# Making the four q units of the sparse attention in the fixed front part and keeping them in DRAM

## The chip, the cores and the metric

The kernel is one program on one core of a Trainium2 chip. The metric is the device time of one execution in microseconds (us). The engines are TensorE (PE, with its weight loads as PEld), VectorE (DVE), ScalarE (ACT), GpSimd (POOL) and SyncE (SP), which here issues most of the DMAs.

## The reference

A transformer block with three parallel mixers and a second block of two layers, all in float32, for 512 tokens of width 1024. What the change touches is the sparse attention (NSA) of the first block and the mLSTM beside it:

```
h = rmsnorm(x, g_pre_mix[l])
z = h @ w_in[l]
q_nsa, kv_nsa, g_nsa, qkv_ml, if_ml, o_ml, q_mem, g_merge = jnp.split(z, offsets, axis=-1)
q = q_nsa.reshape(B, S, NSA_GROUPS, NSA_HPG, NSA_DH)          # 4 groups x 4 heads x 64
o_cmp, p_cmp = nsa_compressed(q, kv[:, :, 0], kv[:, :, 1], ...)  # scores against 31 compressed keys
o_slc = nsa_selected(q, kv[:, :, 2], kv[:, :, 3], top_i, top_ok)
o_win = nsa_window(q, kv[:, :, 4], kv[:, :, 5])
y_nsa = gb[..., 0:1] * o_cmp + gb[..., 1:2] * o_slc + gb[..., 2:3] * o_win
...
h_ml = mlstm_chunkwise(q_m, k_m, v_m, i_pre, logf)            # 4 heads of 128
h_ml = h_ml * lax.rsqrt(jnp.mean(h_ml * h_ml, axis=-1, keepdims=True) + EPS) * ml_head_g
y_ml = jax.nn.sigmoid(o_ml) * h_ml
...
gm = jax.nn.sigmoid(g_merge.reshape(B, S, N_BRANCH, D_MODEL))
y = gm[:, :, 0] * (y_nsa @ w_proj_nsa) + gm[:, :, 1] * (y_ml @ w_proj_ml) + gm[:, :, 2] * (y_mem @ w_proj_mem)
```

## The kernel before, in words

**Units.** Every matrix product goes in units of 256 weight columns. SP loads the unit's weights (1 MB) into one of two buffers `w_raw`; ACT copies them, rounded, to `w_hi`; POOL (DVE in later parts) subtracts to get `w_lo`; PE then makes hi*hi, lo*hi and hi*lo, 48 matmuls of 512 columns for a feature-major unit. Each buffer has two halves that alternate, and every engine does its part in program order: ACT and DVE run the same list of steps as PE, and where a step waits, what stands behind it on that engine waits too.

**The front.** `UNITS` are 22 fixed units (memory keys, compressed, selected and window keys and values, gates, then 14 to 17 `qk`, 18 and 19 `v`, 20 and 21 `o` of the mLSTM). `SCHEDULE` is the order, written by hand, of these units and the steps of the mixers between them. For each mLSTM head h there are `ml_scores` (PE makes one broadcast and four score matmuls; ACT and DVE turn each into decayed, masked scores; the third and fourth matmul wait for the first and second to be masked), `ml_out` (PE, 10 matmuls; DVE makes the reciprocal of the denominator, ACT scales and squares; `m_h` is then counted up, for which the next head's `ml_scores` waits), `ml_gain` and `ml_norm` (two heads each; ACT root, DVE 8 multiplications, `m_y`), and last `ml_turn` (PE turns the result by 16 transposes; ACT and DVE split it into `yml`, counted by `m_lo_s`).

**The loop over 4 groups.** Each turn uses four units: one q unit and three units of the merge gates (two tiles of 128 columns each). PE first makes the q unit (`products`), then 18 of the 144 gate matmuls (`GATE_PRE`), waits until ACT and DVE have split q into `q_stacked` (`q_split`), makes 32 small matmuls against the compressed keys, then 35 attention steps with 3 gate matmuls in each (`GATE_STEP`), then the tail: it turns the compressed probabilities (`c_t`), makes 12 gate matmuls, 16 outputs of the compressed branch, the gate matmuls that are left, and turns `y_tok` when DVE has it ready (`y_done`). `q_stacked` lies in the place of `qk_in`, the key tiles `k_st` in that of `o_ml`.

Of the kernel before, what the change touches and what calls it, by code (L numbers as in the profile page):

```python
# [13 lines left out]
P = 128  # L14
T = 512
# [33 lines left out]
for _name, _count in ROWS:  # L49
# [9 lines left out]
         ("in", C_V, UC, "v"), ("in", C_V + UC, UC, "v"), ("in", C_O, UC, "o"), ("in", C_O + UC, UC, "o")]  # L59
NFIX = len(UNITS)  # L60
FEATURE_MAJOR = ("mem_k", "q_mem", "kc", "vc", "ks", "kw", "qk")
# [7 lines left out]
for _h in range(4):  # L69
    SCHEDULE += [("mem_scores", _h), ("unit", 6 + 2 * _h), ("mem_turn", _h), ("unit", 7 + 2 * _h), ("mem_out", _h)]  # L70
    if _h in (1, 2):
# [3 lines left out]
             ("ml_scores", 0), ("ml_out", 0), ("unit", 19), ("ml_scores", 1), ("ml_out", 1),  # L75
             ("unit", 20), ("ml_gain", 0), ("ml_norm", 0), ("unit", 21), ("ml_scores", 2), ("ml_out", 2), ("ml_scores", 3),
             ("ml_gain", 1), ("ml_out", 3), ("ml_norm", 1), ("ml_turn", 0)]
# [29 lines left out]
GATE_PRE, GATE_STEP = 18, 3  # L107
GATE_EVAC = {8: 0, 16: 1, 24: 2, 32: 3}
# [38 lines left out]
NSA_PER = 31  # L147
# [70 lines left out]
def build(nc, A, const_in, invcount_in, out):  # L218
    with ExitStack() as ctx:
# [48 lines left out]
        kcmp = at("k_cmp", [P, GROUPS, NC], PE0 + 8 * KB + 768)  # L268
# [41 lines left out]
        d_ml = [at(f"decay{i}", [P, T], WK + (41 + 2 * i) * KB - 512) for i in range(2)]  # L310
# [17 lines left out]
        q_st = at("q_stacked", [P, HPG, T], WK, F32R)  # L328
        k_st = [[at(f"k_{name}_{part}_twice", [P, T], WK + (30 + 4 * b + 2 * i) * KB, F32R)
# [54 lines left out]

        g_scratch = nc.dram_tensor("gate_scratch", [GATE_TILES * GROUPS, P, T], F32, kind="Internal").ap()
# [69 lines left out]
        q_high = sem("q_first_high_ready")  # L455
        q_split = sem("q_split_ready")
# [102 lines left out]
        def _(sp):  # L559
# [29 lines left out]
            sp.wait_ge(k_stored, 64)  # L589
            with sp.Fori(0, GROUPS) as g:  # L590
                def gate_load(b):
                    load(g * 2 + (U_NSA // 2 + (b + 1) // 2), (b + 1) % 2, w_in_t[:, :, bass.ds(g * UC + (C_MERGE + b * D), UC)], KT, UC)

                load(g * 2 + U_NSA // 2, 0, w_in_t[:, :, bass.ds(g * UC, UC)], KT, UC)
                gate_load(0)
                gate_load(1)
# [8 lines left out]
                gate_load(2)  # L605
# [57 lines left out]
        def _(act):  # L663
            chain = Chain(act_chain_s)

            def high_in_loop(u2, s, slot):

                act.wait_ge(w_landed[s], u2 * 16 + 16)
                act.wait_ge(w_used, u2 * 2 + (s - 1))
                nc.scalar.activation(w_hi[slot][:, :], raw[s][:, :], ACT.Copy).then_inc(w_hi_ready, 1)  # L670
# [73 lines left out]
            def evacuate(u):  # L744
# [40 lines left out]
                if kind == "qk":  # L785

                    for j in range(2 * (u - 14), 2 * (u - 14) + 2):
# [65 lines left out]
            def ml_turn(_):  # L853
                for h in range(4):
                    act.wait_ge(m_turned, h + 1)
                    nc.scalar.activation(yml[0][:, h, :], bank[h][:, :], ACT.Copy).then_inc(m_hi_s, 1)
# [4 lines left out]
                     "ml_turn": ml_turn}  # L861
# [15 lines left out]
            with act.Fori(0, GROUPS) as g:  # L877
                high_in_loop(g * 2 + U_NSA // 2, 1, 1)
                act.wait_ge(w_used, g * 4 + (U_NSA + 1))
                for h in range(2):  # L880
                    half = slice(DH * h, DH * (h + 1))
                    nc.scalar.activation(q_st[half, h, :], bank[0][half, :], ACT.Copy).then_inc(q_high, 1)
# [28 lines left out]
                for i in range(NS + 2):  # L911
# [19 lines left out]
                ins.then_inc(c_ta, 1)  # L931
                gate_evac(4)
# [218 lines left out]
        def _(pe):  # L1151
# [1184 lines left out]
```

## Time and profile before

| | |
|---|---|
| median of 3 runs | 3069.28 us (3068.79 to 3071.99) |
| the profiled execution | 3068.96 us, span 3067.1 us, mean granted TensorE clock 0.971 |
| PE busy | 2897.8 us, 94% of the span |
| DVE, ACT, POOL busy | 1455.8, 895.2, 333.9 us |
| chain that ended last | PE 72%, issue 16%, POOL 5%, DVE 3% |

The clock column of the views is the share of full speed that TensorE was granted: 1.00 is 2.4 GHz, 0.50 is 1.2 GHz. Idle time in a view is the time that an engine stood before an instruction, with the instruction that released it behind the arrow.

### The profile page before, as it was taken

The page shows a single profiled execution, that of the slowest core. Times are in us where ns is not written, and L with a number is a line of the kernel's source. Part 1 is how long each engine was busy: PE and PEld are TensorE (multiplying, and loading weights), DVE is VectorE, ACT ScalarE, POOL GpSimd, SP SyncE. Part 2 cuts the span into 40 slices and gives each one's busy share as a digit, 9 for nine tenths or more (in the row PEclk, how much of TensorE's full clock was granted, in tenths as well). Part 3 has the DMA queues.
Part 4 walks back from the last instruction along what each step waited for, and adds up shares of the span by engine and source line. Part 5 has one row for each costly group of instructions (what it writes and reads, how often), then busy time and mean ns, then how long its engine had stood idle before and what let it go on. Part 6 is the DMA issues. An engine that isn't in the chain of part 4 may idle for free.

```text
span 3067.1 us, 34757 instructions
## 1 busy us (share of the span) xinstructions
PE 2897.8 (94%) x13510; PEld 2378.6 (78%) x13510; DVE 1455.8 (47%) x2131; ACT 895.2 (29%) x1222; POOL 333.9 (11%) x64
## 2 busy tenths in 40 slices
PE   6988799999899999999999999999999889899997
PEld 6777688888777888778888888878888765588886
DVE  2334354444457453375433644344453389454532
ACT  4333443334233221232222422122222231422221
POOL 4322112111310000000000000000000065100000
PEclk9998899999999999999999999999999999999999
DMA  6222112221442223322232222332222221223222
GB/s 192 91 63 69 55 42 73 80 75 45 147 142 71 96 96 103 103 69 96 96 115 71 91 96 96 103 103 82 96 96 88 77 69 42 69 71 102 95 91 72
DMA packets 255086, 270.55 MB, mean 88 GB/s; under 512 B 5695, under 2 KB 243407, under 8 KB 254858
## 3 DMA queue, kind: packets, MB, share of 16 engines
q1 hardware_dynamic: 250688, 261.87, 26.5%
q10 hardware_dynamic: 4298, 7.36, 0.7%
q8 instruction: 61, 1.00, 0.1%
q14 instruction: 39, 0.32, 0.0%
HBM read 258.72 MB, written 10.49 MB: 88 GB/s over the span
## 4 chain that ended last, share of the span: by engine, by line
PE 72%; issue 16%; POOL 5%; DVE 3%; ACT 2%; DMA 1%; SPq 0%; POOLq 0%; ACTq 0%; DVEq 0%
PE bank L1164 21%; PE bank L1165 21%; PE bank L1166 21%; POOL w_lo L1127 3%; POOL w_lo L1121 3%; PE bank L1658 1%; PE bank L1179 1%; PE bank L1180 1%; PE bank L1181 1%; ACT w_hi L678 1%; PE bank L1192 1%; PE bank L1194 1%; PE bank L1193 1%; PE bank L1309 0%; DVE rstd L2090 0%
## 5 line engine op out<-in xcount | busy, mean ns | idle before, releaser
L1164 PE MATMUL bank<-h_hi,w_hi 128*128 128x512 f32 x2064 | 814.0, 394 | 43.2 <-POOL w_lo L1127 24.6
L1165 PE MATMUL bank<-h_lo,w_hi 128*128 128x512 f32 x2064 | 808.9, 392 | 0.0
L1166 PE MATMUL bank<-h_hi,w_lo 128*128 128x512 f32 x2064 | 808.6, 392 | 0.0
L2046 DVE TENSOR_TENSOR w_lo<-w_raw,w_hi 128x2048 fp32r<-128x2048 f32 (+1 forms) x174 | 386.8, 2225 | 423.3 <-ACT w_hi L678 363.8
L1164 PEld LDWEIGHTS bank<-h_hi,w_hi 128*128 128x128 f32 x2064 | 391.4, 190 | 132.4 <-POOL w_lo L1127 28.8
L1165 PEld LDWEIGHTS bank<-h_lo,w_hi 128*128 128x128 f32 x2064 | 391.1, 190 | 81.9 <-issue 1.2
L1166 PEld LDWEIGHTS bank<-h_hi,w_lo 128*128 128x128 f32 x2064 | 390.8, 189 | 82.2
L678 ACT ACTIVATE w_hi<-w_raw 128x2048 fp32r<-128x2048 f32 (+2 forms) x120 | 218.5, 1825 | 459.8 <-PE bank L1166 412.5
L1164 PE MATMUL bank<-hid_hi,w_hi 128*128 128x512 f32 x880 | 343.4, 390 | 0.0
L1166 PE MATMUL bank<-hid_hi,w_lo 128*128 128x512 f32 x880 | 342.4, 389 | 0.0
L1165 PE MATMUL bank<-hid_lo,w_hi 128*128 128x512 f32 x880 | 342.4, 389 | 0.0
L1127 POOL TENSOR_TENSOR w_lo<-w_raw,w_hi 128x2048 fp32r<-128x2048 f32 x34 | 216.8, 6380 | 1088.4 <-ACT w_hi L678 1088.3
L670 ACT ACTIVATE w_hi<-w_raw 128x2048 fp32r<-128x2048 f32 x114 | 217.8, 1911 | 337.6 <-PE bank L1166 330.1
L971 ACT ACTIVATE gate_tmp<-gate_tmp 128x512 f32<-128x512 f32 x110 | 67.7, 632 | 492.2 <-DVE gate_tmp L2137 492.2
L1164 PEld LDWEIGHTS bank<-hid_hi,w_hi 128*128 128x128 f32 x880 | 165.2, 188 | 34.6 <-issue 0.5
L1165 PEld LDWEIGHTS bank<-hid_lo,w_hi 128*128 128x128 f32 x880 | 165.2, 188 | 34.6 <-issue 0.5
L1166 PEld LDWEIGHTS bank<-hid_hi,w_lo 128*128 128x128 f32 x880 | 165.2, 188 | 34.4
L2145 DVE TENSOR_TENSOR gate_tmp<-gate_tmp,bank 128x512 f32<-128x512 f32 x110 | 75.6, 687 | 238.8 <-PE bank L1166 236.8
L2137 DVE TENSOR_TENSOR gate_tmp<-bank,rstd 128x512 f32<-128x512 f32 x110 | 70.9, 686 | 189.2 <-PE bank L1166 188.9
L1121 POOL TENSOR_TENSOR w_lo<-w_raw,w_hi 128x2048 fp32r<-128x2048 f32 x24 | 110.1, 4591 | 435.0 <-ACT w_hi L670 435.0
L888 ACT ACTIVATE prob<-prob,nsa_stat 128x512 f32<-128x512 f32 (+3 forms) x128 | 71.8, 561 | 157.9 <-DVE nsa_stat L1968 157.9
L1968 DVE CUSTOM_DVE_ANT_0 prob<-bank,const_masks 128x512 f32<-128x512 f32 (+3 forms) x128 | 62.8, 491 | 113.5 <-PE bank L1430 72.5
(366 smaller groups left out, 3431.2 us busy)
## 6 DMA issues: line engine op xcount, KB each, us to landing
w_raw<-in_ffn_w_in_dram SPq DMA_DIRECT2D x88, 1024.0 KB, 5.1
w_raw<-in_w_in_dram SPq DMA_DIRECT2D x32, 1024.0 KB, 5.3
w_raw<-in_ffn_w_out_dram SPq DMA_DIRECT2D x32, 1024.0 KB, 4.9
w_raw<-in_w_ffn_in_dram SPq DMA_DIRECT2D x22, 1024.0 KB, 5.1
w_raw<-in_ffn_w_out_dram SPq DMA_DIRECT2D x16, 768.0 KB, 4.3
w_raw<-in_conv_w_pw_dram SPq DMA_DIRECT2D x12, 1024.0 KB, 5.3
w_raw<-in_w_ffn_down_dram SPq DMA_DIRECT2D x8, 1024.0 KB, 4.9
gate_scratch<-gate_stage ACTq DMA_DIRECT2D x24, 256.0 KB, 2.0
```

The lines of the kernel that those rows point to most:

```text
L670: nc.scalar.activation(w_hi[slot][:, :], raw[s][:, :], ACT.Copy).then_inc(w_hi_ready, 1)
L678: nc.scalar.activation(w_hi[SLOT[u]][:, 0:n], raw[s][:, 0:n], ACT.Copy).then_inc(w_hi_ready, 1)
L888: nc.scalar.activation(prob[i % 4][:, 0:n], prob[i % 4][:, 0:n], ACT.Exp, bias=nmax[:, i:i + 1], scale=-1.0, accum_out=psum_row[:, i:i + 1 ...
L971: nc.scalar.activation(tg[t][:, :], tg[t][:, :], ACT.Silu).then_inc(silu_done, 1)
L1121: nc.gpsimd.tensor_tensor(w_lo[s][:, :], raw[s][:, :], w_hi[s][:, :].bitcast(F32), ALU.subtract).then_inc(w_lo_ready, 1)
L1127: nc.gpsimd.tensor_tensor(w_lo[d][:, :], raw[u % 2][:, :], w_hi[d][:, :].bitcast(F32), ALU.subtract).then_inc(w_lo_ready, 1)
L1164: nc.tensor.matmul(bank[b][:, 0:n], wh, xh, start=first, stop=False)
L1165: nc.tensor.matmul(bank[b][:, 0:n], wh, xl, start=False, stop=False)
L1166: ins = nc.tensor.matmul(bank[b][:, 0:n], wl, xh, start=False, stop=last)
L2046: v.tensor_tensor(w_lo[slot][:, 0:n], raw[s][:, 0:n], w_hi[slot][:, 0:n].bitcast(F32), ALU.subtract).then_inc(w_lo_ready, 1)
L2137: v.tensor_tensor(tg[t][:, :], bank[b + t][:, :], rb[:, :], ALU.mult).then_inc(g_scaled, 1)
L2145: mark(v.tensor_tensor(tg[t][:, :], tg[t][:, :], bank[b + 2 + t][:, :], ALU.mult), up_read, n + (t + 1))
```

## The change

The four q units become fixed units 19, 21, 23 and 25 of the front, between the v and o units. PE makes each of them between an `ml_scores` and its `ml_out` (the fourth between the last `ml_out` and `ml_turn`). ACT and DVE split them into a new buffer `q_stage`, and ACT's queue stores each to DRAM (`q_scratch`, 1 MB). SP loads one back into `q_stacked` per group as soon as the group before has turned its compressed probabilities. The loop's units are now two full gate units and two halves of one (128 columns each), and its turn begins with the small matmuls against the compressed keys, with one gate matmul behind each pair. The split of a group's compressed keys moves from the head of its turn into the turn before, the first group's ahead of `ml_out` of the last head. The core of the diff:

```diff
-         ("in", C_V, UC, "v"), ("in", C_V + UC, UC, "v"), ("in", C_O, UC, "o"), ("in", C_O + UC, UC, "o")]
+         ("in", C_V, UC, "v"), ("in", 0, UC, "q"), ("in", C_V + UC, UC, "v"), ("in", UC, UC, "q"),
+         ("in", C_O, UC, "o"), ("in", 2 * UC, UC, "q"), ("in", C_O + UC, UC, "o"), ("in", 3 * UC, UC, "q")]
...
-             ("ml_scores", 0), ("ml_out", 0), ("unit", 19), ("ml_scores", 1), ("ml_out", 1),
...
+             ("ml_scores", 0), ("unit", 19), ("ml_out", 0), ("q_store", 0), ("unit", 20), ("ml_scores", 1), ("unit", 21), ("ml_out", 1),
...
-GATE_PRE, GATE_STEP = 18, 3
-GATE_EVAC = {8: 0, 16: 1, 24: 2, 32: 3}
+GATE_CMP, GATE_STEP = 1, 3
+GATE_EVAC = {6: 0, 13: 1, 21: 2, 29: 3}
...
@@ SP
+            sp.wait_ge(q_stored, 16)
+            sp.wait_ge(sT_ready, 4 * TT)
+            sp.sem_inc(c_t, 1)
...
-                sp.wait_ge(y_split, g * 2 + 2)
+                gate_load(0, 0, 0, UC)
+                gate_load(0, 1, D, UC)
+
+                sp.wait_ge(c_t, g + 1)
+                sp.dma_start(q_st[:, :, :].rearrange("p h t -> p (h t)").bitcast(F32),
+                             q_scratch[bass.ds(g, 1), :, :].rearrange("a p n -> p (a n)")).then_inc(q_landed, 16)
+                sp.wait_ge(m_y, 16)
...
+                gate_load(1, 0, 2 * D, P)
+                gate_load(1, 1, 2 * D + P, P)
@@ ACT
+            def q_store(n):
+                u = UNIT_OF["q"][n]
+                act.wait_ge(evac_act, u + 1)
+                act.wait_ge(evac_dve, DVE_EVACS[u + 1])
+                act.dma_start(q_scratch[n], q_stage[:, :, :].rearrange("p h t -> p (h t)").bitcast(F32)).then_inc(q_stored, 16)
...
-                act.wait_ge(c_t, g + 1)
+                act.wait_ge(c_t, g + 2)
...
                 ins.then_inc(c_ta, 1)
+                high_in_loop(g * 2 + (U_NSA // 2 + 2), 0, 0)
                 gate_evac(4)
@@ PE
-            pe.wait_ge(m_lo_s, 4)
...
+                        if m < 2:
+                            pe.wait_ge(m_lo_s, m + 1)
...
-                products(0, KT, UC, (h_hi, h_lo), (0, 1))
-                gates(GATE_PRE)
-                pe.wait_ge(q_split, g + 1)
...
+                pe.wait_ge(q_landed, g * 16 + 16)
+                pe.wait_ge(kc_ready, g + 1)
...
+                        gates(GATE_CMP)
@@ DVE
+                elif kind == "q":
+                    if TURN_OF[u] > 0:
+                        dve.wait_ge(q_stored, 16 * TURN_OF[u])
+                    halves = (slice(0, DH), slice(DH, P))
+                    for h in range(2):
+                        link(v.tensor_scalar(q_stage[halves[h], 2 + h, :], b1[halves[h], :], 1.0, None, ALU.mult))
+                    for h in (2, 3, 0, 1):
+                        if h == 0:
+                            dve.wait_ge(evac_act, u + 1)
+                        own, other = halves[h % 2], halves[1 - h % 2]
+                        ins = v.tensor_tensor(q_stage[other, h, :], bank[2 * (u % 2) + h // 2][own, :],
+                                              q_stage[own, h, :].bitcast(F32), ALU.subtract)
```

On ACT, at the end of the front, the rows of the kernel before run from the last head's output (`h_ml`) over the root and the four copies of `ml_turn` to the loop:

```order
L839 ACTIVATE h_ml<-bank,stat 128x128 x4
L841 ACTIVATE ml_junk,stat<-h_ml 128x128 x4
L849 ACT_TABLE_LOAD
L849 ACTIVATE stat<-stat 128x4x2
L856 ACTIVATE yml_hi<-bank 128x512 x4
L877 UNCONDITIONAL_BRANCH
```

and of the changed kernel at the same place:

```order
L863 ACTIVATE h_ml<-bank,stat 128x128 x4
L865 ACTIVATE ml_junk,stat<-h_ml 128x128 x4
L873 ACT_TABLE_LOAD
L873 ACTIVATE stat<-stat 128x4x2
L696 ACTIVATE w_hi<-w_raw 128x2048
L803 ACTIVATE q_stage<-bank 64x512 x2
L886 DMA q_scratch<-q_stage 128x2048
L880 ACTIVATE yml_hi<-bank 128x512 x4
```

Between the root and the copies there now stand the next unit's `w_hi`, the fourth q unit's two copies and its store.

On PE, at the head of the loop's turn, the kernel before has the last of the 18 gate matmuls and then 32 small ones in a row, of which the first rows are

```order
L1403 MATMUL bank<-h_hi,w_lo 128x512
L1424 REGISTER_ALU
L1429 MATMUL bank<-k_cmp_high,q_stacked 128x32
L1430 MATMUL bank<-k_cmp_low,q_stacked 128x32
L1429 MATMUL bank<-k_cmp_high,q_stacked 128x32
L1430 MATMUL bank<-k_cmp_low,q_stacked 128x32
```

and the changed kernel has, behind the 16 transposes of `ml_turn`,

```order
L1403 MATMUL bank<-identity_ones,h_ml 128x128 x16
L1414 UNCONDITIONAL_BRANCH
L1414 ISA
L1453 REGISTER_ALU
L1449 MATMUL bank<-k_cmp_high,q_stacked 128x32
L1450 MATMUL bank<-k_cmp_low,q_stacked 128x32
L1422 ISA
L1426 ISA
L1430 MATMUL bank<-h_hi,w_hi 128x512
L1449 MATMUL bank<-k_cmp_high,q_stacked 128x32
L1450 MATMUL bank<-k_cmp_low,q_stacked 128x32
L1430 MATMUL bank<-h_lo,w_hi 128x512
```

The q unit is gone from the head of the turn, and a gate matmul of 512 columns stands behind each small pair.

## Rows read from the trace of the kernel before

**Rows 1.** The page, part 1.

```profile
PE 2897.8 (94%) x13510; PEld 2378.6 (78%) x13510; DVE 1455.8 (47%) x2131; ACT 895.2 (29%) x1222; POOL 333.9 (11%) x64
```

**Rows 2.** Windows: from head 0's scores to the first group's attention.

```profile
core 0: us, PE busy (x) PEld busy (x) DVE busy (x) ACT busy (x) POOL busy (x), PEclk, DMA share, GB/s
271.50:391.70 120.20, 95.14 (x524) 78.68 (x523) 44.26 (x107) 42.10 (x90) 21.26 (x5) 0.84 0.18 53
```

**Rows 3.** Waits of PE in 271 to 392 us: total, times, longest.

```profile
PE bank L1378 <- DVE h_ml L1890: 7.8, 1, 7.8
PE bank L1357 <- DVE s_ml L1865: 5.3, 6, 1.4
PE bank L1368 <- DVE s_ml L1865: 4.5, 4, 1.2
PE bank L1352 <- ACTq L844: 4.5, 1, 4.5
PE bank L1164 <- DVE yml_lo L1896: 1.8, 1, 1.8
PE bank L1429 <- DVE q_stacked L1926: 1.1, 1, 1.1
```

**Rows 4.** Windows of lowered clock (columns as in rows 2).

```profile
277.30:284.90 7.60, 6.68 (x33) 6.68 (x34) 1.62 (x8) 0.84 (x3) 0.00 (x0) 0.55 0.22 77
342.60:355.50 12.90, 9.96 (x22) 5.36 (x23) 6.28 (x13) 3.50 (x13) 0.00 (x0) 0.50 0.00 0
362.90:373.00 10.10, 5.74 (x17) 4.57 (x18) 5.24 (x15) 5.36 (x7) 1.61 (x1) 0.50 0.13 37
390.40:396.90 6.50, 6.50 (x19) 5.28 (x20) 2.82 (x7) 1.63 (x4) 0.00 (x0) 0.50 0.00 0
489.50:495.50 6.00, 6.00 (x22) 5.33 (x22) 1.53 (x4) 0.81 (x2) 0.00 (x0) 0.50 0.00 0
591.70:594.60 2.90, 2.90 (x8) 2.30 (x7) 1.32 (x4) 0.81 (x2) 0.00 (x0) 0.50 0.00 0
567.80:571.00 3.20, 3.20 (x11) 2.26 (x10) 2.37 (x13) 0.57 (x1) 0.00 (x0) 0.50 0.25 89
```

**Rows 5.** Window of the q unit of group 1 (columns as in rows 2).

```profile
470.92:481.92 11.00, 11.00 (x52) 9.10 (x51) 2.63 (x4) 3.21 (x2) 4.60 (x1) 1.00 0.52 150
```

**Rows 6.** Timeline of DVE and POOL: start, duration, what, idle before.

```profile
321.96 6.57 DVE L1890 SCALAR_TENSOR_TENSOR h_ml<-h_ml,stat,o_ml 128x128 f32<-128x128 f32 x8
323.51 4.61 POOL L1127 TENSOR_TENSOR w_lo<-w_raw,w_hi 128x2048 fp32r<-128x2048 f32 x1 [5.69 <-ACT w_hi L678]
356.90 0.35 DVE L1872 COPY stat<-bank 128x2 f32<-128x2 f32 x2 [2.89 <-PE bank L1368]
363.24 2.19 DVE L1890 SCALAR_TENSOR_TENSOR h_ml<-h_ml,stat,o_ml 128x128 f32<-128x128 f32 x8
818.24 9.47 POOL L1121 TENSOR_TENSOR w_lo<-w_raw,w_hi 128x2048 fp32r<-128x2048 f32 x2 [15.92 <-ACT w_hi L670]
823.22 0.68 DVE L2028 TENSOR_TENSOR merge_gate<-merge_gate,bank 128x512 f32<-128x512 f32 x1
```

**Rows 7.** Timeline of DVE: the split of the first q unit.

```profile
382.78 1.41 DVE L1922 TENSOR_SCALAR q_stacked<-bank 64x512 fp32r<-64x512 f32 x2
384.33 2.94 DVE L1926 TENSOR_TENSOR q_stacked<-bank,q_stacked 64x512 fp32r<-64x512 f32 x4
```

**Rows 8.** Timeline: the tail of group 0 on ACT, DVE and PE.

```profile
457.17 1.92 ACT L670 ACTIVATE w_hi<-w_raw 128x2048 fp32r<-128x2048 f32 x1 [0.71 <-ACT gate_stage L906]
460.31 2.03 ACT L929 ACTIVATE pT_cmp<-bank 31x512 f32<-31x512 f32 x4 [1.23 <-PE bank L1480]
466.85 3.16 DVE L2009 SCALAR_TENSOR_TENSOR y_tok<-bank,nsa_stat,y_tok 128x64 f32<-128x64 f32 x16 [7.66 <-PE bank L1487]
470.07 1.09 PE L1494 MATMUL bank<-identity_ones,y_tok 128*128 128x128 f32 x8 [1.07 <-DVE y_tok L2009]
```

**Rows 9.** The page, part 6: KB of each DMA and us to landing.

```profile
w_raw<-in_w_in_dram SPq DMA_DIRECT2D x32, 1024.0 KB, 5.3
```

More of the change, by code:

```diff
@@ L74 @@
              ("ml_const", 0), ("ml_rows", 0), ("unit", 15), ("unit", 16), ("unit", 17), ("ml_cols", 0), ("unit", 18),
-             ("ml_scores", 0), ("ml_out", 0), ("unit", 19), ("ml_scores", 1), ("ml_out", 1),
-             ("unit", 20), ("ml_gain", 0), ("ml_norm", 0), ("unit", 21), ("ml_scores", 2), ("ml_out", 2), ("ml_scores", 3),
-             ("ml_gain", 1), ("ml_out", 3), ("ml_norm", 1), ("ml_turn", 0)]
+             ("ml_scores", 0), ("unit", 19), ("ml_out", 0), ("q_store", 0), ("unit", 20), ("ml_scores", 1), ("unit", 21), ("ml_out", 1),
+             ("q_store", 1), ("unit", 22), ("ml_scores", 2), ("unit", 23), ("ml_out", 2), ("q_store", 2), ("ml_gain", 0), ("ml_norm", 0),
+             ("unit", 24), ("ml_scores", 3), ("ml_gain", 1), ("first_keys", 0), ("ml_out", 3), ("ml_norm", 1), ("unit", 25), ("q_store", 3), ("ml_turn", 0)]
 U_NSA = NFIX
@@ L143 @@
 K_END = 1656
-NSA_PER = 31
+NSA_PER = 25
 class Chain:
@@ L309, in build @@
         conv_acc = [at(f"conv_acc{i}", [P, T], AR + (58 + 2 * i) * KB) for i in range(2)]
-        d_ml = [at(f"decay{i}", [P, T], WK + (41 + 2 * i) * KB - 512) for i in range(2)]
+        d_ml = [at(f"decay{i}", [P, T], WK + (41 + 2 * i) * KB) for i in range(2)]
         head_g = at("head_g", [P, T], AR + 56 * KB)
@@ L785, in evacuate @@
                 if kind == "qk":
-                    for j in range(2 * (u - 14), 2 * (u - 14) + 2):
+                    for j in range(2 * TURN_OF[u], 2 * TURN_OF[u] + 2):
                         act.wait_ge(conv_done, j + 1)
@@ L855, in ml_turn @@
                     act.wait_ge(m_turned, h + 1)
[L856 removed]
+                    nc.scalar.activation(yml[0][:, h, :], bank[ML_TURN_BANK[h]][:, :], ACT.Copy).then_inc(m_hi_s, 1)
+            def q_store(n):
[3 more added lines that the diff above has]
+                act.dma_start(q_scratch[n], q_stage[:, :, :].rearrange("p h t -> p (h t)").bitcast(F32)).then_inc(q_stored, 16)
             steps = {"mem_scores": mem_scores, "mem_turn": mem_turn, "mem_out": mem_out, "cmp_hidden": cmp_hidden,
@@ L878, in _ @@
                 high_in_loop(g * 2 + U_NSA // 2, 1, 1)
[L879 to L882, printed above, removed]
                 def exp_step(i):
@@ L1777, in unit @@
                     dve.wait_ge(evac_act, u + 1)
-                    for j in range(2 * (u - 14), 2 * (u - 14) + 2):
+                    for j in range(2 * TURN_OF[u], 2 * TURN_OF[u] + 2):
                         acc = conv_acc[j % 2][:, :]
@@ L1904, in _ @@
                     steps[what](n)
-            dve.wait_ge(mask_in_place, 16)
-            for i in range(2):
-                link(v.memset(kc_st[i][:, :].bitcast(F32), 0.0))
             dve.sem_inc(y_split, 2)
```

144 lines of the change are left out of this document (78 added, 66 removed).

## The prediction

> **What bounds the kernel now.** I read the page's busy times first: PE is busy 94% of the span, no other engine half of it [rows 1]. So a change pays only by what it takes from PE's idle time or gives back of its clock. The number of matmuls of full width stays the same. The windows show where there is something to take: from head 0's scores to the first group's attention PE is busy 95.1 of 120.2 us at a mean clock of 0.84 [rows 2]. The waits of PE there add up to 25.0 us: 7.8 before `ml_turn` for the normalised heads, 5.3 within `ml_scores` for masked scores, 4.5 before `ml_out` (1.2 for each of heads 0 to 2 and 0.9 for head 3), 4.5 before the last `ml_scores` for ACT, 1.8 at the loop's head for `yml`, 1.1 for the q split [rows 3]. The windows of lowered clock show the second loss: there PE works at 1.2 GHz, so about half of its busy time in each is lost [rows 4].
>
> **What is removed.** Three q units leave this comparison, since they only change place: a q unit takes 11.0 us at full clock [rows 5], in the loop as in the front. I compare the moment at which the compressed scores of group 0 are done, before and after, for the same amount of matmuls.
>
> Idle time taken away, from rows 3: the waits before `ml_out` of heads 0 to 2 (3.6) get a q unit of 11 us over them, and the masks that they wait for come 1.2 us after the scores. The 4.5 before the last `ml_scores` gets an o unit. The 7.8 before `ml_turn` gets the fourth q unit. The 1.1 for the q split of group 0 goes, and so does the 1.8, in which all four parts of `yml` were waited for. Sum 18.8 us. The 5.3 within `ml_scores` stays.
>
> **What comes back as new waits.** ACT and DVE are in order, and now carry more.
>
> *Before the last scores.* The split of a q unit holds DVE for 4.5 us (382.78 to 387.27) [rows 7] before it can take the denominator of `ml_out`. From there to the root took 356.90 to about 363.0, 6.1 us [rows 6]. So after q unit 23 the root comes at 4.5 + 6.1 = 10.6 us. The 8 multiplications of `ml_norm` follow; free of POOL they take 2.19 us, beside POOL's `w_lo` they took 6.57 [rows 6]. In this place ACT makes the next unit's `w_hi` right behind the root, as in the slow case, so they end at about 17.4. PE needs only `ml_out` (2.5) and o unit 24 (some 11.4 us, a little over a q unit) to be at the last scores at 13.9, and DVE's first argument is wanted 1.1 us later. PE waits some 2.4 us for it, with ACT's tables between sigmoid and exponential 3. What was a step without consequence now delays the scores.
>
> *Before `ml_turn`.* From the last `ml_out` to the last multiplication took 356.90 to 365.43, 8.5 us [rows 6]. Now `w_hi` of the loop's first unit stands right behind the root on ACT, and so POOL lies beside the multiplications again: 8.5 + 4.4 = 12.9, less 11.0 of q unit 25: 1.9 us of wait.
>
> *At the loop's head.* DVE splits q unit 25 only then (4.5), ACT's store waits for that split, and ACT's copies for `yml` are queued behind the store: some 0.4 us for the issue, 0.6 for the first copy, 0.7 for DVE's part. That is 6.3 us after the last multiplication, of which PE fills 2.2 with transposes and the first small pair; then its first gate matmul waits 4.1 us. New waits: 3 + 1.9 + 4.1 = 9.0. Idle time net: 18.8 - 9.0 = 9.8 us.
>
> **The clock in this stretch.** Lost before, by rows 4: 3.3 at head 0's scores, the same again at head 1's (a window alike), 5.0 at 342.6, 2.9 at 362.9, 3.3 at 390.4: 17.8 us. In each case PE had stood still or had only sparse matmuls just before. After the change these stretches are followed by dense units, yet the scores with their inner waits stay as they are. I keep 2.5 us for head 0, 2.5 for head 1 and 1 for head 2 (between nothing and the 3.3 seen), 3.5 for the last head with its longer wait, and 2.5 at the loop's head: 12. Gain 6, and between 0 and 13 if these choices are all wrong one way. The front gives 9.8 + 6 = 16.
>
> **The loop's heads of groups 1 to 3.** The q split's 1.1 us goes three times (the same row stands in each group's waits): 3.2. The clock fell behind the 32 small matmuls of each group: 6.0 us busy at half in group 1, 2.9 in groups 2 and 3 alike [rows 4]: 3.0 + 1.45 + 1.45 = 5.9 lost. With a full matmul behind each small pair PE is dense for half of this place; in the short attention steps it is about as dense and its clock holds. I expect most of the 5.9 back, but not surely; the fall in the tail (567.8 to 571.0, 1.6 us lost [rows 4]) stays. I count 8 us of 3.2 + 5.9.
>
> **What is new there, costed at nothing.** The q load is issued at `c_t`, when the transposes of the compressed probabilities are done, at about 460.2 in group 0. PE turns `y_tok` from 470.07 to 471.16 [rows 8], 11 us after `c_t`; a load of 1 MB lands in 5.3 us [rows 9]. Cover 5.5 us; late, it costs what is over, in each of three groups. The key loads behind it have the small matmuls and 16 gate matmuls as well, some 7 us more. The first gate unit's `w_hi` moves from before `c_t` (457.17) to behind ACT's four copies (2.03 us) [rows 8]: 2.1 + 1.9 + 4.6 of POOL puts `w_lo` at 8.7 us after `c_t`, 2.3 us before it is wanted. Its half units are made earlier and smaller. Four stores and four loads of 1 MB more lie on queues that are idle most of the time.
>
> This new place puts POOL's 4.6 us (from 4.1 to 8.7) beside DVE's 16 operations on `y_tok` (from 6.6 on) [rows 8]. Where both inputs are in SBUF, DVE stood still until POOL was done; an operation with one input in a bank took its usual 0.68 us at 823.22, inside POOL's 818.24 to 827.71 [rows 6]. The 16 read a bank, so I count nothing; if they were held, `y_done` would come 2.1 us later in each of 4 groups, 8 us in all. The Trainium skill (SBUF — State Buffer, Who interferes with whom) says that a DVE instruction with two SBUF inputs contends with a GpSimd instruction that reads SBUF, and one with at most one does not. These 16 have `y_tok` and a per-partition factor in SBUF; if the factor counted as an input, that rule would give the 8 us, and if it does not, it gives the row's nothing. `h_ml` at 321.96, which was held, has two tensors there.
>
> **Sum.** 16 + 8 = 24 us. Against the profiled execution's 3069.0 that is 3045; the median of the runs is 0.3 us higher. I take 3046. A difference under 0.2% (6 us) can't be told from none by a measurement of this kernel.
>
> **The rivals.**
>
> *Likeliest, 0.5*: as above, 3046, its own range 3039 to 3052.
>
> *The clock comes back nearly whole, 0.18.* Dense units let it fall only at the last head and at the loop's head: the front gives 9.8 + 12, the heads 9.1: 31 to 33 us, 3037. For it: the q unit at 470.92 ran at 1.00 throughout [rows 5]. Against: at head 0 the clock fell at once after the scores, before `ml_out`'s wait was over.
>
> *More is given back, 0.25.* The clock still falls behind the compressed scores in each group (the 5.9 is not gained), and the front's falls last as long as before (6 is not gained): 24 - 5 - 6 = 13, 3056. For it: the small matmuls are still 32, and the wait of 4.1 us stands just before them in group 0. The 8 us of a held `y_tok` would give 3054 alone.
>
> *No change, 0.04*: the waits net out and the clock gives nothing, for instance if the root of the last head is held by more than I see; 3066.
>
> *Slower, 0.03.* The q load comes late at the head of every group. For that SP's queue must hold it, with two weight loads ahead of it, until far after `c_t`. To eat 24 us in three groups it must be 8 us late in each, so land 19 us after `c_t`, against 5.3 for such a load. From there on the kernel is slower; at 22 us it would be at 3078. For it: only that SP's order puts this load behind two waits for free weight buffers. Against: those buffers are free some steps before `c_t`.
>
> **The numbers.** Cases at 3037, 3046 and 3056 hold over nine tenths; the range from 3033 to 3058 leaves about one in ten on either side. Faster by over 0.2%: 0.92; within: 0.05; slower: 0.03.
>
> **What would show it.** Right: no wait before `ml_out` of heads 0 to 2 and none before the last `ml_scores`; PE's waits within the last head's scores near 5 to 6 us in all; waits of about 2 us before `ml_turn` and of about 4 us at the first gate matmul, for `yml`; no wait at `q_landed` in groups 1 to 3; clock at 1.00 behind their compressed scores. Wrong: a wait for weights (`w_lo`) or for q at a group's head, `y_tok` longer than 3.2 us for its 16, or falls of the clock in each turn's head as before. The sum would be most wrong in the clock, which makes up 11 of the 24.

## The result

The changed kernel takes **3049.68 us** (median of 4 runs, 3049.34 to 3050.25); the kernel before, measured with it, 3069.18. The ratio is 0.9935, with an interval of 0.9917 to 0.9952. So it is faster by 0.65%, 19.5 us, where 23 were forecast (3046); the time lies in the likeliest case's own range.

### The profile page after: what moved, and what is told of

The parts are those of the page before. It is cut to its first block, busy times and chain, and to the rows that moved or that the text cites. A ratio compares the mean times of both kernels' runs of the same rounds, so it can differ in the third digit from the quotient of the medians.

```text
span 3048.0 us, 34807 instructions
## 1 busy us (share of the span) xinstructions
PE 2889.1 (95%) x13510; PEld 2375.7 (78%) x13510; DVE 1462.4 (48%) x2134; ACT 896.1 (29%) x1227; POOL 334.7 (11%) x68
## 4 chain that ended last, share of the span: by engine, by line
PE 75%; issue 15%; POOL 5%; DVE 3%; ACT 2%; DMA 1%; SPq 0%; POOLq 0%; ACTq 0%; DVEq 0%
PE bank L1189 22%; PE bank L1191 22%; PE bank L1190 22%; POOL w_lo L1152 3%; POOL w_lo L1146 2%; PE bank L1686 1%; PE bank L1204 1%; PE bank L1205 1%; PE bank L1206 1%; PE bank L1217 1%; PE bank L1219 1%; PE bank L1218 1%; ACT w_hi L696 1%; PE bank L1334 0%; DVE rstd L2126 0%
## 5 line engine op out<-in xcount | busy, mean ns | idle before, releaser
L696 ACT ACTIVATE w_hi<-w_raw 128x2048 fp32r<-128x2048 f32 (+2 forms) x124 | 226.1, 1828 | 458.4 <-PE bank L1191 411.6
L1152 POOL TENSOR_TENSOR w_lo<-w_raw,w_hi 128x2048 fp32r<-128x2048 f32 x38 | 235.2, 6195 | 1135.4 <-ACT w_hi L696 1135.4
L688 ACT ACTIVATE w_hi<-w_raw 128x2048 fp32r<-128x2048 f32 (+1 forms) x114 | 211.0, 1851 | 336.0 <-PE bank L1191 327.8
L1146 POOL TENSOR_TENSOR w_lo<-w_raw,w_hi 128x2048 fp32r<-128x2048 f32 (+1 forms) x24 | 92.4, 3851 | 368.9 <-ACT w_hi L688 368.9
```

The source lines that it names most:

```text
L688: nc.scalar.activation(w_hi[slot][:, 0:n], raw[s][:, 0:n], ACT.Copy).then_inc(w_hi_ready, 1)
L696: nc.scalar.activation(w_hi[SLOT[u]][:, 0:n], raw[s][:, 0:n], ACT.Copy).then_inc(w_hi_ready, 1)
L1146: nc.gpsimd.tensor_tensor(w_lo[s][:, 0:n], raw[s][:, 0:n], w_hi[s][:, 0:n].bitcast(F32), ALU.subtract).then_inc(w_lo_ready, 1)
L1152: nc.gpsimd.tensor_tensor(w_lo[d][:, :], raw[u % 2][:, :], w_hi[d][:, :].bitcast(F32), ALU.subtract).then_inc(w_lo_ready, 1)
```

## The profile after

The page of the changed kernel, span and busy times:

```profile
span 3048.0 us, 34807 instructions
PE 2889.1 (95%) x13510; PEld 2375.7 (78%) x13510; DVE 1462.4 (48%) x2134; ACT 896.1 (29%) x1227; POOL 334.7 (11%) x68
```

The span is 19.1 us shorter than before. The waits of PE of the changed kernel, window 271 to 430 us, which answer to [rows 3] (total, times, longest):

```profile
PE bank L1382 <- DVE s_ml L1905: 9.3, 8, 3.6
PE bank L1430 <- DVE yml_lo L1950: 3.1, 1, 3.1
PE bank L1403 <- DVE h_ml L1930: 2.0, 1, 2.0
PE bank L1393 <- DVE s_ml L1905: 0.9, 1, 0.9
```

L1382 is `ml_scores`, L1393 `ml_out`, L1403 `ml_turn`, L1430 the gate products. The four make 15.3 us, for 25.0 of before [rows 3]. (One more, 0.7 us for `probT`, belongs to group 0's attention.) The waits before `ml_out` of heads 0 to 2 are gone, and so are the 4.5 for ACT's queue and the q split; the 7.8 before `ml_turn` is 2.0.

Windows of the changed kernel: three stages (head 0's scores to the first selected scores of group 0; the cycles from group 0 to 1 and from 1 to 2), then five places of lowered clock. The first and the last five answer to [rows 2, 4].

```profile
core 0: us, PE busy (x) PEld busy (x) DVE busy (x) ACT busy (x) POOL busy (x), PEclk, DMA share, GB/s
273.01:413.69 140.68, 125.47 (x665) 105.33 (x665) 61.24 (x127) 54.08 (x101) 39.66 (x9) 0.89 0.32 105
413.69:501.89 88.20, 85.28 (x537) 75.17 (x536) 42.09 (x159) 38.36 (x96) 12.49 (x4) 0.95 0.23 72
501.89:587.65 85.76, 82.85 (x537) 73.19 (x536) 42.34 (x159) 38.36 (x96) 13.65 (x5) 0.98 0.26 79
...
279.00:283.00 4.00, 4.00 (x13) 3.09 (x12) 0.66 (x3) 1.56 (x1) 2.36 (x1) 0.58 0.37 132
340.00:344.00 4.00, 3.59 (x10) 2.98 (x11) 1.87 (x7) 2.12 (x3) 1.04 (x1) 0.57 0.46 160
374.00:382.00 8.00, 6.49 (x27) 5.85 (x27) 4.78 (x18) 0.69 (x2) 0.00 (x0) 0.57 0.61 187
395.00:415.70 20.70, 17.62 (x65) 15.53 (x63) 7.39 (x13) 5.27 (x7) 4.53 (x1) 0.51 0.49 153
487.50:494.00 6.50, 6.50 (x20) 5.21 (x20) 3.16 (x16) 0.29 (x1) 2.52 (x1) 0.50 0.78 223
```

What the reader is to see is the row of 395.00. The clock falls at the loop's head as before [rows 4], but now stays at 1.2 GHz for 20.7 us instead of 6.5. The other places are shorter: nothing at head 1, some 4 us at heads 0 and 2.

**Where the 19.1 us came from.** Marks in the trace serve for all kernels below: S is head 0's first `ml_scores`, K the first product with `k_sel` of each group, M the first product of the merge, W the first of `w_out`. The stretch from S to K0 is called the front below, each stretch from one K to the next a cycle. In brackets is length times (1 - PEclk), a measure of what the lower clock cost.

| kernel | to S | S to K0 | K0 to K1 | K1 to K2 | K2 to K3 | K3 to M | M to W | W to end |
|---|---|---|---|---|---|---|---|---|
| before | 271.4 | 120.2 (19.2) | 100.7 (4.0) | 98.9 (4.0) | 98.9 (3.0) | 81.8 | 101.3 | 2193.8 |
| changed | 273.0 | 140.7 (15.5) | 88.2 (4.4) | 85.8 (1.7) | 85.8 (1.7) | 81.3 | 100.4 | 2192.8 |

In the changed kernel three q units of 11.0 us [rows 5] stand ahead of K0 and one of them less in each later cycle. With 33.0 us taken off, S to K0 gained 12.5, of which 0.5 is two gate products that now come later; the three cycles gained 1.5, 2.1 and 2.1, together 5.7; from K3 on there are 2.4 more, and 1.6 was lost before S, in code that the change leaves alone. (The stretch to S lies between 270.7 and 273.5 us in the kernels below, which all share its program; so 1.6 is within its scatter.)

## The experiments

My theory after this: the idle time went as forecast, and the missing part is clock, lost because PE waits 3.1 us for `yml` just before the sparse stretch at the loop's head; in the groups the gate matmuls between the small ones keep the clock. The rivals: the sparse stretch (the small pairs with one gate matmul behind each) itself holds the clock down, wait or no wait; in the groups it is the end of the wait for the q split that helps, not the gate matmuls; and the new places of the gate evacuations cost something that I had not priced.

Four kernels ran on one chip with the kernel before at 3070.62, four more (one of them the changed kernel unchanged) beside 3069.85, and three beside 3070.79. Single executions of one kernel lie up to 9 us apart, and each row of stages is one execution. What each gave:

| kernel | median us | ratio to before | to S | S to K0 | K0 to K1 | K1 to K2 | K2 to K3 | M to W |
|---|---|---|---|---|---|---|---|---|
| e1_turn_first | 3053.64 | 0.9945 [0.9933, 0.9957] | 273.5 | 144.1 (17.3) | 88.4 (4.4) | 85.7 (1.7) | 85.7 (1.7) | 100.0 |
| e2_high_early | 3046.47 | 0.9924 [0.9911, 0.9936] | 270.7 | 138.4 (13.8) | 87.2 (3.5) | 85.8 (1.7) | 85.7 (1.7) | 100.3 |
| e3_gates_apart | 3046.47 | 0.9923 [0.9910, 0.9935] | 272.4 | 136.9 (12.3) | 85.7 (1.7) | 85.7 (1.7) | 85.7 (1.7) | 102.4 |
| e4_no_cover | 3056.06 | 0.9955 [0.9942, 0.9968] | 271.5 | 147.4 (20.6) | 88.3 (4.4) | 85.7 (1.7) | 85.8 (1.7) | 100.3 |
| changed, again | 3047.84 | 0.9930 [0.9916, 0.9943] | 272.3 | 140.6 (14.1) | 88.3 (4.4) | 85.8 (1.7) | 85.8 (1.7) | 100.5 |
| e6_turn_first_again | 3039.11 | 0.9896 [0.9881, 0.9911] | 273.4 | 131.9 (7.9) | 85.6 (0.0) | 85.0 (0.0) | 87.3 (3.5) | 101.3 |
| e7_all_three | 3039.52 | 0.9904 [0.9889, 0.9919] | 272.9 | 128.1 (6.4) | 87.9 (4.4) | 86.9 (2.6) | 87.1 (3.5) | 100.5 |
| e8_keys_late | 3053.24 | 0.9945 [0.9932, 0.9959] | 271.9 | 144.1 (17.3) | 88.2 (4.4) | 85.8 (1.7) | 85.8 (1.7) | 99.8 |
| e9_late_places | 3052.99 | 0.9945 [0.9931, 0.9958] | 272.6 | 137.6 (12.4) | 88.9 (4.4) | 88.1 (3.5) | 86.4 (1.7) | 100.6 |
| e10_turn_and_high | 3034.24 | 0.9879 [0.9864, 0.9894] | 271.3 | 128.0 (6.4) | 87.2 (1.7) | 85.8 (1.7) | 85.8 (1.7) | 100.2 |
| e11_turn_late_places | 3042.49 | 0.9904 [0.9889, 0.9919] | 272.4 | 125.9 (5.0) | 89.5 (3.6) | 86.4 (1.7) | 88.1 (3.5) | 103.1 |

### Covers taken away: e4

```
-("ml_scores", 0), ("unit", 19), ("ml_out", 0), ...   (and heads 1, 2 alike)
+("ml_scores", 0), ("ml_out", 0), ("unit", 19), ...
```

> The changed kernel, with ml_out of heads 0 to 2 right behind its scores and the q unit after it, as the v and o units stood before; the last head as it is. The q units are still made in front, but cover nothing. Theory A: the three waits of 1.2 us come back (3.6) and the clock falls longer behind heads 0 and 1 (1.5 each): 3054 to 3057. Less by some, since the denominator then comes before the q unit and not behind its split: the last scores' wait of 3.6 us may shrink by up to 2.2. Rival B: place in the front makes no difference, most of the gain is in the groups' heads: 3050 to 3051.

The wait of `ml_out`, e4, 271 to 430 us:

```profile
PE bank L1393 <- DVE s_ml L1905: 4.5, 4, 1.2
```

The waits of heads 0 to 2 are back (1.2, 1.2 and 0.9 us; head 3 has 1.2), and S to K0 is 6.7 us longer. The wait within the last scores is shorter in turn (7.1 for `s_ml` in all, where the changed kernel has 9.3), so idle time grew by 1.4 us only, and 5.3 is clock: an uncovered wait of 1.2 us costs little by itself and more by the fall behind it. Theory A holds.

### The turn first: e1 and e6

Both put `ml_turn` ahead of q unit 25's evacuation on ACT and DVE, so that `yml` no longer queues behind the q split and store. In e1 ACT's signal that lets the gate products have their bank still stood behind the store; e6 moves it ahead.

```
 ACT, DVE:  -evacuate(25); q_store(3); ml_turn(0)
            +ml_turn(0); evacuate(25); q_store(3)
 e6, ACT:   +act.sem_inc(gt_copied, 2)      ahead of ml_turn
```

> The changed kernel, with ACT and DVE doing ml_turn's copies before the split and the store of the fourth q unit (PE's order as it was). Theory A: the 3.1 us before the first gate matmul is DVE's split (4.5 us) and ACT's store standing ahead of the parts of yml. So the wait falls to under 0.5 us, and since PE no longer stands still just before the 32 small matmuls, the clock is back at 1.00 some 3 to 7 us sooner than at 415: 3 us of idle and 3 to 6 of clock, 3041 to 3044. Rival B: the clock had already fallen at 395, before that wait, in the wait for ml_turn, and the small matmuls keep it low whatever stands before them: only the 3 us, 3046 to 3047. Rival C: the first w_lo (or the q load) is late next and takes the wait's place: 3049.

> As e1_turn_first, but ACT counts the gate banks free (gt_copied, two counts) before ml_turn; in e1 these counts stood behind the store, and the first gate matmul waited 6.4 us for them instead of 3.1 for yml. Theory A (the split and the store ahead of the copies of yml make the wait): wait at the first gate matmul under 0.5 us, 3.1 us of idle gone, 0 to 5 of clock; 3 to 8 us under r_after. Rival: something third holds it (the first w_lo, the q load) and the wait stays above 2 us.

e1 told nothing of the theory, since one wait took the place of the other. This is its row, 271 to 430 us:

```profile
PE bank L1434 <- ACTq L908: 6.4, 1, 6.4
```

In e6 no wait for `yml` is left, and the clock falls for 4 us only. Its waits in 271 to 400 us, and the window of the fall at the loop's head:

```profile
PE bank L1386 <- DVE s_ml L1909: 9.3, 8, 3.6
PE bank L1407 <- DVE h_ml L1934: 2.0, 1, 2.0
PE bank L1397 <- DVE s_ml L1909: 0.9, 1, 0.9
...
395.00:399.00 4.00, 4.00 (x23) 3.83 (x21) 2.52 (x4) 3.18 (x6) 0.00 (x0) 0.57 0.48 147
```

S to K0 is 8.8 us shorter: 3.1 of wait and 5.7 of clock. The changed kernel that ran on e6's own chip waited longer there:

```profile
PE bank L1430 <- DVE yml_lo L1950: 4.1, 1, 4.1
```

Against it e6's front is 8.7 us shorter, 4.1 of wait and 4.6 of clock. So the sum of the two is firm, and how it divides is not: the place of lowered clock began at 395.0 us in the first profile and only at 397.8 in this one, and so PE reached the wait sooner. The sparse stretch is the same in both kernels, so the rival that it holds the clock down by itself falls: with the wait ahead of it, it stays at 1.2 GHz to its end, without the wait PE is back at 2.4 GHz inside it. The other runs bear this out. In all seven profiles with a wait just ahead of or inside the pairs (2.4 to 6.4 us: the changed kernel twice, e1, e2, e4, e8, e9) the clock was low at the end of the pairs; in the three without (e6, e10, e11) it was not. The time is 8.7 us below the changed kernel's on the same chip.

### The high halves early: e2

```
-high_next(24)   behind ml_out(2) and the root      +high_next(24)   behind evacuate(23)
-high_next(25)   behind the last root               +high_next(25)   ahead of ml_out(3)
```

> The changed kernel, with ACT making w_hi of unit 25 right behind q unit 23's copies, and w_hi of unit 26 before ml_out of the last head, so that POOL's w_lo no longer lies beside the 8 multiplications of ml_norm. Theory A: each norm then takes 2.2 us and not 6.6. The wait within the last head's scores falls from 3.6 to about 1.4, that before ml_turn from 2.0 to 0, that for yml grows by up to 1 (DVE's split of the q unit still starts when PE is done with it): 3 to 4 us, with 0 to 3 of clock, 3043 to 3047. Rival B: the norm is not held by POOL; the waits stay and the time stays at 3049.7.

DVE's 8 multiplications in the changed kernel, and POOL's `w_lo` beside them (two timelines: start, us):

```profile
364.56 6.48 DVE L1930 SCALAR_TENSOR_TENSOR h_ml<-h_ml,stat,o_ml 128x128 f32<-128x128 f32 x8
366.10 4.52 POOL L1152 TENSOR_TENSOR w_lo<-w_raw,w_hi 128x2048 fp32r<-128x2048 f32 x1 [18.55 <-ACT w_hi L696]
387.51 6.49 DVE L1930 SCALAR_TENSOR_TENSOR h_ml<-h_ml,stat,o_ml 128x128 f32<-128x128 f32 x8
389.06 4.80 POOL L1152 TENSOR_TENSOR w_lo<-w_raw,w_hi 128x2048 fp32r<-128x2048 f32 x1 [18.44 <-ACT w_hi L696]
```

The same in e2, where POOL has done or not begun:

```profile
365.25 2.19 DVE L1934 SCALAR_TENSOR_TENSOR h_ml<-h_ml,stat,o_ml 128x128 f32<-128x128 f32 x8
385.77 2.19 DVE L1934 SCALAR_TENSOR_TENSOR h_ml<-h_ml,stat,o_ml 128x128 f32<-128x128 f32 x8
380.59 4.61 POOL L1156 TENSOR_TENSOR w_lo<-w_raw,w_hi 128x2048 fp32r<-128x2048 f32 x1 [21.61 <-ACT w_hi L696]
```

The 4.3 us come back each time, and the wait before `ml_turn` is gone. But the wait within the last scores is 2.8 where it was 3.6, not the expected 1.4. POOL's first `w_lo`, moved forward, now lies beside a small operation of DVE on the denominators of `ml_out`, with both inputs in SBUF:

```profile
355.87 3.12 DVE L1917 SCALAR_TENSOR_TENSOR stat<-stat 128x4 f32<-128x4 f32 x1
354.36 4.62 POOL L1156 TENSOR_TENSOR w_lo<-w_raw,w_hi 128x2048 fp32r<-128x2048 f32 x1 [9.10 <-ACT w_hi L696]
```

In the changed kernel it took 0.16 us; here it ends when POOL does. The root on ACT comes 3.0 us later by it, counted from S, and with it ACT's loads of the tables for sigmoid and exponential, on which the last scores now wait. The edit moved the collision more than it removed it. And the wait for `yml` was 4.5, for the 3.1 and 4.1 of the two profiles of the changed kernel, because the q split and store that stand ahead of it now begin no earlier than PE has made the q unit; S to K0 gained only 2.3.

### The gate products apart: e3 and e7

```
+gates(16 * GATE_CMP)             ahead of the wait for q and the small matmuls
 for each small pair: ...
-    gates(GATE_CMP)
```

> The changed kernel, with each group's 16 gate matmuls ahead of the 32 small ones instead of one behind each pair. It asks what the interleaving does to the clock. Theory A: it holds the clock at 1.00 in groups 1 to 3, so apart the clock falls there again behind the small ones (1.5 to 3 us each as before the change), 4 to 6 us; but in group 0, where the clock is low already when they start, 16 dense ones bring it back early, 3 to 5 us to the good: 3049 to 3052. Rival B: what made the clock fall before was the 1.1 us wait for q, not the bare small ones: groups 1 to 3 stay at 1.00 and group 0 gains: 3045 to 3047.

In e3 the 32 small matmuls stand bare again, as in the kernel before, but without its wait of 1.1 us for the q split ahead of them. The cycle K0 to K1 of e3 has the clock of the changed kernel's later groups:

```profile
409.38:495.07 85.69, 82.97 (x538) 73.15 (x538) 42.43 (x158) 38.34 (x96) 12.13 (x4) 0.98 0.26 81
```

So the groups' clock can hold without a gate matmul between the small pairs, which was the reason that the prediction gave. Gate products ahead of the small ones had stood in the kernel before too; what is left as a difference is the wait for the q split and the q unit ahead of it. But e7 below has the same heads as e3, and there the clock fell again. e3 also gains 3.8 in the front, all of it clock, for the waits are as before it. At group 0's head e3's 16 gate matmuls stand in one piece behind the wait for `yml` (3.3 us there), and over the place the clock is 0.77, where the changed kernel has 0.51 over nearly the same:

```profile
395.00:416.00 21.00, 17.15 (x89) 14.14 (x87) 10.81 (x21) 8.94 (x16) 4.55 (x1) 0.77 0.50 151
```

The two medians (3046.47 here, 3049.68 and 3047.84 for the changed kernel) can't be told apart: the intervals of the ratios overlap. What is said of e3 rests on the stages of one profile.

> The three edits together: ml_turn ahead of the fourth split on ACT and DVE (with the counts mended), w_hi of units 25 and 26 early, each group's 16 gate matmuls ahead of the small ones. If they add up: no wait before ml_turn and for yml, 2.8 within the last scores, clock back at 1.00 within some 7 us of the loop's head; the stretch from the first scores to the first group's attention falls from 140.7 to 128 to 131, the first turn from 88.2 to 85.7: 12 to 15 us under r_after. If the clock takes them back, 8.

e7 joins e6, e2 and e3 and comes out level with e6. Its front is 3.8 us shorter, its cycles are 2.3, 1.9 and -0.2 longer. The fall at group 1's head began among the bare small matmuls, which no wait preceded (a timeline, and the window):

```profile
486.97 0.26 PE L1456 MATMUL bank<-k_cmp_high,q_stacked 128*128 128x32 f32 x1
487.24 0.38 PE L1456 MATMUL bank<-k_cmp_high,q_stacked 128*128 128x32 f32 x1
...
487.00:494.00 7.00, 7.00 (x24) 5.94 (x24) 2.81 (x7) 1.60 (x4) 2.48 (x1) 0.51 0.28 75
```

Group 2 of e7 has one right behind its small matmuls (575.9 to 579.3 us), and a third lies in group 0's tail (476.9 to 480.3). With a gate matmul between the pairs, the heads of groups 1 to 3 show no fall, neither within the pairs nor right behind them, in any of ten profiles (the changed kernel twice, e1, e2, e4, e6, e8 to e11). Bare and with the 1.1 us wait (before) all three fell; bare and without it (e3, e7) two of six. So the interleaving is not always needed and may still be what made the heads safe. These runs don't part it from the end of the wait.

### The keys late: e8

```
-("ml_gain", 1), ("first_keys", 0), ("ml_out", 3), ...  ("ml_turn", 0)]
+("ml_gain", 1), ("ml_out", 3), ...  ("ml_turn", 0), ("first_keys", 0)]
```

> The second part of the change undone: the first group's compressed keys are split behind ml_turn on DVE, not ahead of the last ml_out. Theory A: PE then waits for them at the loop's head until DVE has made the four parts of yml (2.9 us) and the keys (0.8), instead of 3.1 for the first part of yml: 3 us more of idle there, 3 to 5 us over r_after. Rival: the wait for yml covers it, under 1 us.

The wait at the loop's head in e8, 271 to 430 us:

```profile
PE bank L1449 <- DVE k_cmp_low L1937: 6.2, 1, 6.2
```

6.2 us for 3.1 and 4.1, and S to K0 3.4 to 3.5 us longer. That is what the small edit of `first_keys` is worth; the clock, already low for the whole place, had little more to lose.

### The places of the evacuations: e9 and e11

```
-GATE_EVAC = {6: 0, 13: 1, 21: 2, 29: 3}
+GATE_EVAC = {8: 0, 16: 1, 24: 2, 32: 3}
```

> The changed kernel, with the four evacuations of the gate unit in each group put back from tiles 6, 13, 21, 29 to 8, 16, 24, 32. Question: PE waits 2.2 to 3.6 us a group for probT on ScalarE, where before it waited 1.6 to 1.8. Theory A, the new places of the evacuations make ScalarE late for probT: the waits come back to about 1.7 us a group, 3 to 5 us less in all, 3043 to 3046 us. Rival B, what makes ScalarE late is the high half of a W tile, which now falls at other points of the group: no difference, within 1 us of the changed kernel. Rival C, the last evacuation comes too late for the bank: up to 2 us more.

Waits of PE in 430 to 760 us, first the changed kernel, then e9:

```profile
PE bank L1488 <- ACT probT L922: 10.9, 19, 0.9
```

```profile
PE bank L1430 <- POOL w_lo L1146: 9.2, 4, 2.3
PE bank L1488 <- ACT probT L922: 5.5, 11, 0.7
```

The mechanisms of A and of C were both at work; the time that A gave was not met. The old places halve the waits for `probT`, 5.4 us over this window. But the last half unit of weights is made on ACT right behind the last evacuation, and its `w_lo` now comes 2.3 us late in each of four groups; behind three of these four waits the clock falls once more (first at 476.7 us), and K1 to K2 is 2.3 us longer. The new places are the better bargain. My C named the bank; it was the weights.

> The kernel of e6_turn_first_again with the evacuation places 8, 16, 24, 32 instead of 6, 13, 21, 29. If the places make the waits for probT, 3 to 5 us less than e6_turn_first_again, 3034 to 3036; if they do not, 3039 again, within 1 us; if the clock of the groups' heads hangs on what else moves, up to 4 us more.

e11 came out between e6 and the changed kernel, 3.4 us above e6 where 3 to 5 less was the first theory, with the same 9.2 us of waits for `w_lo`. Its front is the shortest of all, 125.9, for a reason that has nothing to do with its edit (below, under what was not expected).

### Turn first and high halves early: e10

This is e7 with the gate products between the small matmuls again.

> The changed kernel with the last turn ahead of the o unit (as in e6_turn_first_again) and the last two high halves made earlier (as in e2_high_early), but the gate products still between the compressed scores. Together these two were in e7_all_three with the gate products apart, which came out at 3039.5, no better than the turn alone at 3039.1: there the front was 3.8 us shorter and the groups' heads fell to the lower clock again. Theory A, the gate products apart cost the groups' heads their clock once the turn stands first: without them the front keeps most of the 3.8 us and groups 1 and 2 stay at 85.0 to 85.6 us, so 3035 to 3037. Rival B, it is where the group begins in time that decides on the clock, not what stands at its head: the heads fall again, 3038 to 3041.

Waits of PE in e10, 271 to 399 us, above 0.2 us:

```profile
PE bank L1389 <- DVE s_ml L1912: 8.4, 8, 2.7
PE bank L1400 <- DVE s_ml L1912: 1.2, 1, 1.2
```

Neither `ml_turn` nor `yml` is waited for. The front is that of e7 (128.0 and 128.1), and the cycles are 0.7, 1.1 and 1.3 us shorter: the gate products apart, which had kept the clock in e3, cost 3 us here, as far as one profile of each can say. (Of the 5.3 us between the two medians the rest is not in these stages: 1.6 us lies before S, where the programs are the same.) e10 is the fastest version, **3034.24 us**, 0.9879 of the kernel before, and beats both.

## Why the prediction was right, and where its sizes were off

**Idle time of the front: right.** The forecast was 25.0 less 9.8 net, 15.2 us; the trace shows 15.3, in part by luck, since two misses of 1 us cancel. Of the new waits, the last scores' was put at 3 and `s_ml` shows 9.3 for the 5.3 of before, so 4.0; before `ml_turn` 1.9 was forecast and 2.0 measured; for `yml` 4.1 and 3.1 (4.1 in the second profile, which makes 16.3 in all). The mechanism was the forecast one: in both places POOL's `w_lo` held DVE's multiplications (6.48 and 6.49 us), which e2 undid. The sign "near 5 to 6 us in all" within the last head's scores came out at 4.2 (3.6 and 0.6).

**Clock of the front: the sum's mis-sized term.** The prediction kept 12 us lost, of them "2.5 at the loop's head". Taking busy time at half clock, head 0 lost 1.7 (2.5 forecast), head 1 nothing (2.5), head 2 1.5 (1), the last head 2.8 (3.5), and the loop's head 17.62 busy at 0.51, 8.6 us. Together 14.6 for 12; by the lengths, 12.0 us won in the front less 9.7 of idle time leaves 2.3 of clock for the forecast 6. I had seen the 4.1 us wait and named it as a danger in "more is given back", but priced the clock behind it as if dense work followed. What follows is small pairs and single gate matmuls, 14 us of it. e6 priced the term by taking the wait away: 5.7 of clock beside the 3.1 (4.6 beside 4.1 by the second profile). That the time still came out within 4 us of the forecast owes something to head 1 and the last head, which lost less than was put down for them.

**The groups' heads: direction right, 5.7 for 8, and the reason open.** The q split's 1.1 is gone in each, 3.2 as forecast, and no q load is waited for. Of the clock's 5.9, "most" was expected back; the three cycles show 11.0 before and 7.8 after, so 3.2. The falls behind the small matmuls are gone in all three groups, as forecast. But the cycle from group 0 to 1 has a new one: 6.50 us busy at 0.50, as much as the fall that went [rows 4]. It lies in group 0's tail, where the kernel before had none. It begins within the outputs of the compressed branch and is over before the first small pair (494.53):

```profile
484.24 4.44 PE L1515 MATMUL bank<-v_cmp,pT_cmp 31*128 x32
```

The prediction said that the tail's falls stay, and did not count one in group 0. Whether the gate matmul behind each pair is what removed the falls at the heads is open: e3 did without it, e7 did not. The rest (0.7 us by this reckoning, 1.1 by the waits) is the balance of the other waits. Those for `probT` grew from 5.1 to 8.7 us over the three cycles, which the prediction did not price at all, and 2.5 of smaller ones went (1.1 of them before `y_tok`'s turn). e9 showed that the new evacuation places make the waits for `probT`, and that the old ones would now cost more.

**Costed at nothing: right.** No wait for q, for `w_lo` or before `y_tok`'s turn. DVE's 16 operations on `y_tok` in group 0 took their 3.16 us, as in [rows 8], although POOL's `w_lo` lay beside the first of them until 490.02:

```profile
488.80 3.16 DVE L2044 SCALAR_TENSOR_TENSOR y_tok<-bank,nsa_stat,y_tok 128x64 f32<-128x64 f32 x16 [8.31 <-PE bank L1515]
485.50 4.52 POOL L1146 TENSOR_TENSOR w_lo<-w_raw,w_hi 128x2048 fp32r<-128x2048 f32 x1 [8.08 <-ACT w_hi L688]
```

By the Trainium skill (SBUF — State Buffer, Who interferes with whom) a DVE instruction with at most one SBUF input does not contend with GpSimd. The trace agrees, if the per-partition factor is not counted as a second input.

**Everything else.** Group 3, the merge and what follows gained 2.4 us and the stretch before S lost 1.6, together 0.8 us that no step of the prediction has. 12.5 + 5.7 + 2.4 - 1.6 = 19.0 of the span's 19.1.

## What to carry to other kernels

Price a wait by what follows it: 3.1 us of idle time (4.1 in the second profile) ahead of sparse matmuls cost 8.8 with the clock. With 16 wide matmuls in one piece behind a wait of 3.3 (e3, front 136.9, against e6's 131.9) it cost 5.0; without a wait the two orders have the same front (e7 and e10). When work is put on top of a wait, look at which in-order engine carries its evacuation and what is queued behind it; here the order of two steps on ACT and DVE was worth nearly half as much as the whole change (8.7 and 19.5 us). Gains of the clock need not add: by the stages of their profiles, an edit that helped alone (e3) hurt beside others (e7 against e10), so such edits have to be measured in the version they will live in.

## What the runs showed of the hardware that was not expected

**The same pattern of matmuls ran for long at either level of the clock.** The timeline of PE of the changed kernel, a small pair and a gate matmul at group 0's head and the same at group 1's:

```profile
400.30 0.79 PE L1430 MATMUL bank<-h_hi,w_hi 128*128 128x512 f32 x1 [3.08 <-DVE yml_lo L1950]
400.89 0.23 PE L1449 MATMUL bank<-k_cmp_high,q_stacked 128*128 128x32 f32 x1
400.96 0.38 PE L1450 MATMUL bank<-k_cmp_low,q_stacked 128*128 128x32 f32 x1
401.17 0.77 PE L1430 MATMUL bank<-h_lo,w_hi 128*128 128x512 f32 x1
```

```profile
495.21 0.48 PE L1430 MATMUL bank<-h_lo,w_hi 128*128 128x512 f32 x1
495.53 0.18 PE L1449 MATMUL bank<-k_cmp_high,q_stacked 128*128 128x32 f32 x1
495.56 0.26 PE L1450 MATMUL bank<-k_cmp_low,q_stacked 128*128 128x32 f32 x1
495.67 0.47 PE L1430 MATMUL bank<-h_hi,w_lo 128*128 128x512 f32 x1
```

A step took 0.87 us at 1.2 GHz and 0.46 at 2.4. In group 0, where the clock was low before it and the wait stood in front, the pattern ran at the lower level to its end (413.7), in group 1 at the upper to its end (502). In e6, without a wait in front, the clock rose within the same pattern at 399. So a low clock does not by itself stay low there. A longer wait did not mean a longer fall either: 20.5 us of lowered clock went with the wait of 3.1, 17.1 with the one of 4.1. What exactly decides on it stays open: e6 had no fall at all in two cycles and a longer one at 648 to 655 us in the third, with nothing different there in the program.

**Who gets to go first, DVE or POOL, is not settled by the program.** e9 runs the program of the changed kernel up to K0, and e11 that of e6. In all four POOL's `w_lo` starts 1.54 or 1.55 us after DVE's first multiplication. In the changed kernel DVE was held (6.48, POOL 4.52, above). In e9 DVE came through and POOL took half a microsecond longer:

```profile
364.25 2.19 DVE L1930 SCALAR_TENSOR_TENSOR h_ml<-h_ml,stat,o_ml 128x128 f32<-128x128 f32 x8
365.79 5.03 POOL L1152 TENSOR_TENSOR w_lo<-w_raw,w_hi 128x2048 fp32r<-128x2048 f32 x1 [18.56 <-ACT w_hi L696]
```

In e9 that happened at the first of the two places, in e11 at both (2.19 and POOL 5.04, 2.19 and 5.09), in the seven other profiles that have the two side by side (the changed kernel twice, e1, e3, e4, e6, e8) at neither. It shortened the last scores' wait from 3.6 to 1.6 us. The short fronts of e9 and e11 (137.6 and 125.9 beside 140.7 and 131.9) come with it, as the only difference that I found up to K0: 2.3 and 3.4 us of them are waits, the rest clock. So part of what the table shows for e9 and e11 is luck of one execution. e2, e7 and e10 don't depend on it, because there these two do not meet.
